# Expert down weights read as one run per partition, hidden units dealt out to tiles with a step of four

## The chip, the cores and the metric

The kernel runs on one core of a Trainium2 chip. The metric is the time of one execution in microseconds (us); the median of three runs counts. Engines are named as the profile names them: PE is TensorE (PEld its weight loads), DVE VectorE, ACT ScalarE, POOL GpSimd, SP SyncE.

## The reference

Two layers work on 256 tokens of width 1024, in float32. A layer is a mixer (one input projection, three kinds of heads, an output projection, a residual) and then a mixture of 32 SwiGLU experts of inner width 512, of which each token uses two. For one expert the reference computes

```
(silu(xb @ w_gate[e]) * (xb @ w_up[e])) @ w_down[e]     # xb (tokens, 1024)
# w_gate[e], w_up[e]: (1024, 512)    w_down[e]: (512, 1024)
```

and the results are summed per token with the router's weights. The sum over the 512 inner units in the last product may be taken in any order, if the activations and the rows of w_down go in the same order.

## The kernel before

All experts are computed, each on up to 32 gathered token rows (CAP = 32). Each expert is a unit; four units (UG = 4) make a group, and a layer has 8 groups. A unit needs three loads of 2 MB: gate, up and down. They go into a ring of six slots in SBUF, three for even units and three for odd ones, so that two units are held at a time. The first four units of a layer borrow other buffers (`FIRST`), and two of the down loads are made in halves (`half_down`).

All loads are issued by SP, in order. `unit` waits until TensorE has done the up part of unit i-2 (`gu_ps`), issues gate and up of unit i, waits until the down part of unit i-2 is done (`ye_ps`), and issues down of unit i. The loads of gate and up take eight neighbouring rows of 512 numbers to a partition, 16 KB in one piece. The load of down takes rows p, 128+p, 256+p and 384+p to partition p, four pieces of 4 KB (L400).

On TensorE, `experts` (L583) runs a group: gather the tokens (L589), turn the weights of the routing (L594), then for each unit the "up" part and the "down" part, and at the end the scatter (L631). The up part (L606) has 8 steps k over the model width and in each four matmuls j side by side: matmul j works on 32 columns of the array and computes 128 inner units, for gate and for up at once. Its moving operand is 2 x 128 numbers, the blocks `P * j:P * j + P` of gate and of up; its output has the 32 tokens on partitions 32j to 32j+31 and the units on 256 columns. ACT and DVE make the activation (L889, L1161 to L1167), TensorE transposes it (L611), ACT copies it to SBUF as `actT` (L892), and the down part (L623) multiplies it: block j of actT with rows j of the down tile, which are those inner units that matmul j has computed. L896 and L1171 copy the result out. The order is "up, down, up, down" in most groups; the first group of a layer has up parts ahead of down parts (`OVERLAPPED`).

Each float32 matmul that is no transpose stands in the trace as two records, one for each of two passes. The 32 matmuls of an up part are 64 records, in 16 steps of four records side by side. TensorE's clock has two levels, 1.2 and 2.4 GHz; the profile gives the granted clock as a share of 2.4 GHz.

The one other strided read on TensorE is in `stream_rows` (L848), which has blocks of x transposed by L580 with a step of 8 numbers (32 bytes) from one element to the next; for the mixer the same line transposes blocks of h, and L696 blocks of q and k, that are contiguous. In these transposes the data are the operand that is loaded as weights.

Of the kernel before, what the change touches and what calls it, by code (L numbers as in the profile page):

```python
# [13 lines left out]
ds = bass.ds  # L14

P = 128
# [40 lines left out]
def hybrid_trunk(nc, a, out):  # L57
# [16 lines left out]
    KT = D // P  # L74
# [30 lines left out]
    with ctx:  # L105
        def sb(name, shape, dt=F32):
            return ctx.enter_context(nc.sbuf_tensor(name, shape, dt))
# [5 lines left out]
        ring = sb("ring", [P, R + 1, SLOT])  # L113
# [129 lines left out]
        def slots_of(i):  # L243

            return (3, 4, 5) if i % 2 == 0 else (0, 1, 2)
# [4 lines left out]
        def slot(s):  # L250
            if s == IN_MAPS:
                return maps[:, :, :].rearrange("p m n -> p (m n)")
            if s == IN_WORK:
                return work[:, 0:8, :].rearrange("p m n -> p (m n)")
            return ring[:, s, :]

        def down_tiles(s, half_in_ht=False):

            tiles = slot(s).rearrange("p (j n) -> p j n", j=4)
            early = hT[:, :, :].rearrange("p (j k) t -> p j (k t)", j=2)  # L260
            return [(early if half_in_ht and j < 2 else tiles)[:, j, :] for j in range(4)]
# [100 lines left out]
        def _(e):  # L362
# [22 lines left out]
            for l in range(DEPTH):  # L385
                for c0, name in ((NE, "group"), (0, "expert")):
                    n = a[f"router_{name}_b"].shape[1]
# [3 lines left out]
            for l in range(DEPTH):  # L391
                w_out = a["w_out"][l:l + 1].rearrange("l (k p) n -> p (l k) n", k=KT)

                def part(full, s, ex, n):

                    if n < 2:
                        src = a[("expert_w_gate", "expert_w_up")[n]][l:l + 1, ds(ex, 1)].rearrange("l e (p k) n -> p (l e k n)", k=KT)
                        e.dma_start(slot(s), src).then_inc(full[s].sem, 16)
                    else:
                        src = a["expert_w_down"][l:l + 1, ds(ex, 1)].rearrange("l e (j p) n -> p (l e j) n", p=P)  # L400
                        e.dma_start(slot(s).rearrange("p (j n) -> p j n", j=4), src).then_inc(full[s].sem, 16)

                def half_down(dst, s, ex, half):

                    src = a["expert_w_down"][l:l + 1, ds(ex, 1)].rearrange("l e (j p) n -> p (l e j) n", p=P)
                    e.dma_start(dst, src[:, 2 * half:2 * half + 2, :]).then_inc(ring_full[s].sem, 16)

                def unit(full, S, turn, i, ex):

                    sg, su, sd = slots_of(i)  # L410
                    e.wait_ge(S.gu_ps.sem, S.gu_ps.after(turn, i - 1))
                    part(full, sg, ex, 0)
                    part(full, su, ex, 1)
                    e.wait_ge(S.ye_ps.sem, S.ye_ps.after(turn, i - 1))
                    part(full, sd, ex, 2)
# [37 lines left out]

                e.wait_ge(log_ps.sem, log_ps.after(l, 1))
                half_down(hT[:, :, :].rearrange("p (j k) t -> p j (k t)", j=2), IN_HT, 3, 0)

                e.wait_ge(main.gu_ps.sem, main.gu_ps.after(first, 1))
# [4 lines left out]
                part(ring_full, FIRST[3][1], 3, 1)  # L462
                e.wait_ge(main.ye_ps.sem, main.ye_ps.after(first, 2))
                half_down(slot(IN_MAPS).rearrange("p (j n) -> p j n", j=4)[:, 2:4, :], IN_MAPS, 3, 1)
                part(ring_full, slots_of(4)[2], 4, 2)
                for i in range(1, UG):
# [6 lines left out]
                with e.If(count > 0):  # L473
                    with e.Fori(0, count) as t:

                        e.wait_ge(main.x_added.sem, main.x_added.after(l * GROUPS + GROUPS - 1, 0))
                        for i in range(UG):
                            ex = e.value_load(xinfo[0:1, l:l + 1, ds(t * UG + (2 + i), 1)], min_val=0, max_val=NE - 1)
# [90 lines left out]
        def _(e):  # L569
# [13 lines left out]
            def experts(S, turn, order, slots_of, loaded):  # L583

                e.wait_ge(S.sel_ok.sem, S.sel_ok.after(turn, 1))
                for half in range(2):
                    for k in range(4):
                        for i in range(TI):
                            last = T.matmul(bank[half][:, k * P:k * P + P], h[:, i, 4 * half + k, :], sel[:, i, :],  # L589
                                            start=(i == 0), stop=(i == TI - 1))  # L590
                    last.then_inc(S.gath_ps.sem, 1)
                e.wait_ge(S.gat_ok.sem, S.gat_ok.after(turn, 1))
                for i in range(TI):
                    last = T.transpose(bank[2][:, i * P:i * P + P], gat[:, i, :], ident[:, :])  # L594
                last.then_inc(S.gat_ps.sem, 1)
                for part, i in order:
                    sg, su, sd = slots_of(i)
                    if part == "up":
                        e.wait_ge(S.full[sg].sem, loaded(sg, i))
                        e.wait_ge(S.full[su].sem, loaded(su, i))  # L600
                        gate_up = ring[:, sg:su + 1:su - sg, :].rearrange("p a (k n) -> p a k n", k=KT)
                        for k in range(KT):
                            if i == 0 and k % 4 == 0:
                                e.wait_ge(S.xg_ok.sem, S.xg_ok.after(turn, 1 + k // 4))
                            for j in range(4):
                                last = T.matmul(bank[GU_BANK[i % 2]][CAP * j:CAP * j + CAP, 0:2 * P], xg[:, k, CAP * i:CAP * i + CAP],  # L606
                                                gate_up[:, :, k, P * j:P * j + P], start=(k == 0), stop=(k == KT - 1))
                        last.then_inc(S.gu_ps.sem, 1)
                        continue
                    e.wait_ge(S.act_ok.sem, S.act_ok.after(turn, i + 1))  # L610
                    T.transpose(bank[3][:, 0:P], actv[i % 2], ident[:, :]).then_inc(S.at_ps.sem, 1)  # L611
                    if i:
                        e.wait_ge(S.ye_act.sem, S.ye_act.after(turn, i))
                        e.wait_ge(S.ye_dve.sem, S.ye_dve.after(turn, i))
                    e.wait_ge(S.full[sd].sem, loaded(sd, i))
                    e.wait_ge(S.at_sb.sem, S.at_sb.after(turn, i + 1))
                    early = order is OVERLAPPED and i == UG - 1
                    if early:
                        e.wait_ge(S.full[IN_HT].sem, loaded(IN_HT, i))
                    down = down_tiles(sd, early)  # L620
                    for j in range(4):
                        for q in range(4):
                            last = T.matmul(bank[5][CAP * q:CAP * q + CAP, 0:2 * P], actT[:, CAP * j:CAP * j + CAP],  # L623
                                            down[j][:, 2 * P * q:2 * P * q + 2 * P], start=(j == 0), stop=(j == 3))
                    last.then_inc(S.ye_ps.sem, 1)
                e.wait_ge(S.gat_sb.sem, S.gat_sb.after(turn, 1))
                e.wait_ge(S.ye_act.sem, S.ye_act.after(turn, 4))
                e.wait_ge(S.ye_dve.sem, S.ye_dve.after(turn, 4))
                for n in range(4):
                    i, half = n // 2, n % 2  # L630
                    T.matmul(bank[(6, 7, 0, 1)[n]][:, :], gatT[:, i * P:i * P + P], ye[:, half * 512:half * 512 + 512],  # L631
                             start=True, stop=True).then_inc(S.scat_ps.sem, 1)

            for l in range(DEPTH):
# [141 lines left out]
                for hd in range(HA):  # L776
                    last = T.matmul(bank[5][:, hd * DV:hd * DV + DV], wT[:, hd, :], av[:, 0, hd * DV:hd * DV + DV],
                                    start=True, stop=True)
# [84 lines left out]
                T.matmul(bank[5][:, 2 * NE:3 * NE], ones[:, :], picks[:, 1, :], start=False, stop=True).then_inc(rank_ps.sem, 1)  # L863

                experts(main, l * GROUPS, OVERLAPPED, lambda i: FIRST[i], lambda s, i: ring_full[s].after(l, 16 * loads(s, i)))
                def turn_loaded(g):
                    return lambda s, i: ring_full[s].after(l, 16 * (loads(s, UG - 1) + i // 2 - 1)) + g * 32

                with e.Fori(1, GROUPS - 1) as g:
                    experts(main, l * GROUPS + g, IN_TURN, slots_of, turn_loaded(g))  # L870
                count, prior = extra_groups(e, l)
                with e.If(count > 0):
                    with e.Fori(0, count) as t:
                        e.wait_ge(main.x_added.sem, main.x_added.after(l * GROUPS + GROUPS - 1, 0))
                        experts(extra, prior + t, IN_TURN, slots_of, lambda s, i: xring_full[s].after(prior + t, 16 * (i // 2 + 1)))
# [737 lines left out]
```

## Time and profile before

| | |
|---|---|
| median of three runs | 1299.38 us (1297.89 to 1301.31) |
| the profiled execution, its own time | 1301.28 us |
| its span in the profile | 1299.5 us |
| mean granted TensorE clock | 0.874 |
| busy: PE, DVE, ACT, POOL | 913.4, 496.4, 183.9, 25.9 us |
| moved by DMA | 442.05 MB in 78306 packets |

Busy times are unions of the records of an engine. A DMA packet is one contiguous piece that one of the 16 DMA engines moves; the profile counts packets under 512 B, under 2 KB and under 8 KB, each count including the smaller ones. The chain that ended last is followed back from the last instruction, at each step to what released it.

### The profile page before, as it was taken

The page shows a single profiled execution, that of the slowest core. Times are in us where ns is not written, and L with a number is a line of the kernel's source. Part 1 is how long each engine was busy: PE and PEld are TensorE (multiplying, and loading weights), DVE is VectorE, ACT ScalarE, POOL GpSimd, SP SyncE. Part 2 cuts the span into 40 slices and gives each one's busy share as a digit, 9 for nine tenths or more (in the row PEclk, how much of TensorE's full clock was granted, in tenths as well). Part 3 has the DMA queues.
Part 4 walks back from the last instruction along what each step waited for, and adds up shares of the span by engine and source line. Part 5 has one row for each costly group of instructions (what it writes and reads, how often), then busy time and mean ns, then how long its engine had stood idle before and what let it go on. Part 6 is the DMA issues. An engine that isn't in the chain of part 4 may idle for free.

```text
span 1299.5 us, 19555 instructions
## 1 busy us (share of the span) xinstructions
PE 913.4 (70%) x8133; PEld 554.1 (43%) x8133; DVE 496.4 (38%) x1245; ACT 183.9 (14%) x544; POOL 25.9 (2%) x63
## 2 busy tenths in 40 slices
PE   5999876667566575656679989757666664665565
PEld 4558453434334343434354574534333342433242
DVE  6666462332323231413147663623323131323222
ACT  2324111110010101110013241010010100010000
POOL 2001000000000000000000020000000000000000
PEclk9999877988888888988689999778878798889888
DMA  7825549899999999999964253498999999999995
GB/s 253 325 97 186 203 163 364 342 420 425 423 422 420 421 424 422 423 423 416 405 241 163 94 205 142 188 397 348 423 422 420 420 423 423 423 423 419 421 422 212
DMA packets 78306, 442.05 MB, mean 340 GB/s; under 512 B 9120, under 2 KB 12208, under 8 KB 61872
## 3 DMA queue, kind: packets, MB, share of 16 engines
q1 hardware_dynamic: 78256, 441.36, 83.7%
q8 instruction: 34, 0.56, 0.2%
q14 instruction: 16, 0.13, 0.0%
HBM read 440.30 MB, written 1.05 MB: 340 GB/s over the span
## 4 chain that ended last, share of the span: by engine, by line
PE 52%; DMA 31%; DVE 11%; issue 2%; ACT 2%; SPq 1%; DVEq 0%; ACTq 0%
DMA ring<-in_expert_w_up 31%; PE bank L606 15%; PE bank L648 8%; PE bank L623 6%; PE bank L657 5%; PE bank L715 4%; PE bank L589 4%; PE bank L631 4%; DVE work L1163 2%; PE bank L679 1%; DVE work L1171 1%; PE bank L580 1%; PE bank L611 1%; ACT work L892 1%; ACT maps L948 1%
## 5 line engine op out<-in xcount | busy, mean ns | idle before, releaser
L606 PE MATMUL bank<-ring,work 128*32 128x256 f32 x4096 | 286.8, 442 | 115.0 <-DMA ring<-in_expert_w_up 114.6
L606 PEld LDWEIGHTS bank<-ring,work 128*32 128x32 f32 x4096 | 163.0, 127 | 236.3 <-issue 161.5
L623 PE MATMUL bank<-ring,work 128*32 128x256 f32 x1856 | 149.6, 477 | 26.6 <-ACT work L892 26.6
L1161 DVE TENSOR_SCALAR work<-work 128x128 f32<-128x128 f32 x64 | 14.5, 227 | 365.8 <-ACT work L889 365.8
L1171 DVE COPY work<-bank 32x256 f32<-32x256 f32 x128 | 54.3, 424 | 206.1 <-PE bank L623 205.2
L611 PE MATMUL bank<-ident,work 128*128 128x128 f32 x64 | 22.4, 349 | 128.4 <-DVE work L1167 128.4
L648 PE MATMUL bank<-ring,hT 128*128 128x512 f32 x256 | 112.4, 593 | 0.0
L623 PEld LDWEIGHTS bank<-ring,work 128*32 128x32 f32 x1856 | 76.7, 133 | 76.6 <-issue 64.1
L589 PE MATMUL bank<-work,h 128*128 128x128 f32 x512 | 73.1, 311 | 40.7 <-DVE work L1141 40.7
L589 PEld LDWEIGHTS bank<-work,h 128*128 128x128 f32 x512 | 70.1, 223 | 52.6 <-DVE work L1141 52.6
L611 PEld LDWEIGHTS bank<-ident,work 128*128 128x128 f32 x64 | 9.3, 145 | 158.6 <-DVE work L1167 156.2
L657 PE MATMUL bank<-hT,ring 128*128 128x256 f32 x320 | 75.3, 397 | 0.8 <-DVE hT L1213 0.8
L631 PE MATMUL bank<-work 128*128 128x512 f32 x128 | 60.9, 620 | 17.2 <-DVE work L1171 17.2
L896 ACT ACTIVATE work<-bank 32x256 f32<-32x256 f32 x128 | 47.8, 373 | 175.1 <-PE bank L623 174.4
L648 PEld LDWEIGHTS bank<-ring,hT 128*128 128x128 f32 x256 | 47.7, 190 | 54.9 <-issue 54.5
L889 ACT ACTIVATE work<-bank 128x128 f32<-128x128 f32 x64 | 17.8, 278 | 356.2 <-PE bank L606 356.2
L657 PEld LDWEIGHTS bank<-hT,ring 128*128 128x128 f32 x320 | 63.4, 200 | 10.6 <-DVE hT L1213 1.2
L1163 DVE RECIPROCAL work<-work 128x128 f32<-128x128 f32 x64 | 61.0, 953 | 2.2
L715 PE MATMUL bank<-ring,hT 128*128 128x512 f32 x128 | 58.1, 610 | 2.8 <-ACT hT L1041 2.8
L1176 DVE TENSOR_TENSOR x<-bank,x 128x512 f32<-128x512 f32 x64 | 44.3, 691 | 30.7 <-PE bank L631 30.7
L631 PEld LDWEIGHTS bank<-work 128*128 128x128 f32 x128 | 23.8, 196 | 49.7 <-issue 49.7
L715 PEld LDWEIGHTS bank<-ring,hT 128*128 128x128 f32 x128 | 24.8, 198 | 32.0 <-issue 32.0
(258 smaller groups left out, 683.6 us busy)
## 6 DMA issues: line engine op xcount, KB each, us to landing
ring<-in_expert_w_gate SPq DMA_DIRECT2D x64, 2048.0 KB, 18.0
ring<-in_expert_w_up SPq DMA_DIRECT2D x64, 2048.0 KB, 22.3
ring<-in_expert_w_down SPq DMA_DIRECT2D x58, 2048.0 KB, 21.9
ring<-in_w_in SPq DMA_DIRECT2D x12, 2048.0 KB, 19.2
ring<-in_w_out SPq DMA_DIRECT2D x4, 2048.0 KB, 8.0
maps<-in_expert_w_down SPq DMA_DIRECT2D x2, 2048.0 KB, 12.7
work<-in_expert_w_down SPq DMA_DIRECT2D x2, 2048.0 KB, 8.3
ring<-in_w_in SPq DMA_DIRECT2D x2, 1024.0 KB, 5.5
```

The costliest lines, as they stand in the source:

```text
L589: last = T.matmul(bank[half][:, k * P:k * P + P], h[:, i, 4 * half + k, :], sel[:, i, :], start=(i == 0), stop=(i == TI - 1))
L606: last = T.matmul(bank[GU_BANK[i % 2]][CAP * j:CAP * j + CAP, 0:2 * P], xg[:, k, CAP * i:CAP * i + CAP], gate_up[:, :, k, P * j:P * j + P] ...
L611: T.transpose(bank[3][:, 0:P], actv[i % 2], ident[:, :]).then_inc(S.at_ps.sem, 1)
L623: last = T.matmul(bank[5][CAP * q:CAP * q + CAP, 0:2 * P], actT[:, CAP * j:CAP * j + CAP], down[j][:, 2 * P * q:2 * P * q + 2 * P], start= ...
L631: T.matmul(bank[(6, 7, 0, 1)[n]][:, :], gatT[:, i * P:i * P + P], ye[:, half * 512:half * 512 + 512], start=True, stop=True).then_inc(S.sc ...
L648: last = T.matmul(bank[b][:, :], hT[:, k, i * P:i * P + P], W[:, k, :], start=(k == 0), stop=(k == KT - 1))
L657: last = T.matmul(bank[b][:, c * SEQ:c * SEQ + SEQ], W[:, k, c0:c0 + P], hT[:, k, :], start=(k == 0), stop=(k == KT - 1))
L715: last = T.matmul(bank[2 * i + half][:, :], mixT[:, k, i * P:i * P + P], W[:, k, :], start=(k == 6), stop=(k == 3))
L896: last = A(ye[CAP * i:CAP * i + CAP, 2 * P * q:2 * P * q + 2 * P], bank[5][CAP * q:CAP * q + CAP, 0:2 * P], ACT.Copy)
L1163: V.reciprocal(r, r).then_inc(c.step(), 1)
L1171: last = V.tensor_copy(ye[CAP * i:CAP * i + CAP, 2 * P * q:2 * P * q + 2 * P], bank[5][CAP * q:CAP * q + CAP, 0:2 * P])
L1176: TT(xs, bank[(6, 7, 0, 1)[n]][:, :], xs, ALU.add).then_inc(S.x_added.sem, 1)
```

## The change

The rows of the down weights go to partitions as 4p, 4p+1, 4p+2 and 4p+3, so that each partition reads 16 KB in one piece (8 KB in the half loads). To match it, matmul j of the up part computes the inner units 4q+j, q = 0 to 127, in place of 128j+q: it reads the gate and up tiles with a step of four numbers (16 bytes). Nothing else differs; no instruction is added or removed on any engine, and gate and up are loaded as before.

```diff
                     else:
-                        src = a["expert_w_down"][l:l + 1, ds(ex, 1)].rearrange("l e (j p) n -> p (l e j) n", p=P)
+                        src = a["expert_w_down"][l:l + 1, ds(ex, 1)].rearrange("l e (p j) n -> p (l e j) n", p=P)
                         e.dma_start(slot(s).rearrange("p (j n) -> p j n", j=4), src).then_inc(full[s].sem, 16)
...
                 def half_down(dst, s, ex, half):
-                    src = a["expert_w_down"][l:l + 1, ds(ex, 1)].rearrange("l e (j p) n -> p (l e j) n", p=P)
+                    src = a["expert_w_down"][l:l + 1, ds(ex, 1)].rearrange("l e (p j) n -> p (l e j) n", p=P)
...
-                        gate_up = ring[:, sg:su + 1:su - sg, :].rearrange("p a (k n) -> p a k n", k=KT)
+                        gate_up = ring[:, sg:su + 1:su - sg, :].rearrange("p a (k n j) -> p a k j n", k=KT, j=4)
...
                                 last = T.matmul(bank[GU_BANK[i % 2]][CAP * j:CAP * j + CAP, 0:2 * P], xg[:, k, CAP * i:CAP * i + CAP],
-                                                gate_up[:, :, k, P * j:P * j + P], start=(k == 0), stop=(k == KT - 1))
+                                                gate_up[:, :, k, j, :], start=(k == 0), stop=(k == KT - 1))
```

## Rows read from the trace of the kernel before

**Rows 1.** The page: engine shares, and DMA in 40 slices of the span.

```profile
PE 913.4 (70%) x8133; PEld 554.1 (43%) x8133; DVE 496.4 (38%) x1245; ACT 183.9 (14%) x544; POOL 25.9 (2%) x63
...
DMA  7825549899999999999964253498999999999995
```

**Rows 2.** The page: the chain that ended last, by engine.

```profile
PE 52%; DMA 31%; DVE 11%; issue 2%; ACT 2%; SPq 1%; DVEq 0%; ACTq 0%
```

**Rows 3.** Windows: the two steady stretches (clock, DMA share, GB/s last).

```profile
254.93:632.71 377.78, 238.83 (x2710) 141.61 (x2711) 107.50 (x252) 35.88 (x109) 0.00 (x0) 0.85 1.01 421
901.00:1277.88 376.88, 237.76 (x2710) 132.89 (x2711) 107.53 (x252) 35.95 (x110) 0.00 (x0) 0.86 1.01 421
```

**Rows 4.** The chain by time (start us, us, what), steady stretch of layer 0.

```profile
374.05 20.00 DMA ring<-in_expert_w_up
...
394.19 5.68 PE bank L606 x64
...
402.90 1.97 PE bank L623 x32
...
417.47 3.63 PE bank L606 x64
...
424.14 1.93 PE bank L623 x32
426.08 3.49 PE bank L606 x64
...
610.36 22.21 DMA ring<-in_expert_w_up
```

**Rows 5.** DMA from 254 to 633 us: packets, then issues with median landing.

```profile
DMA packets 20698, 159.74 MB, mean 421 GB/s; under 512 B 1216, under 2 KB 1216, under 8 KB 14191
...
ring<-in_expert_w_gate SPq DMA_DIRECT2D x25, 2048.0 KB, 18.8
...
ring<-in_expert_w_down SPq DMA_DIRECT2D x25, 2048.0 KB, 22.5
```

**Rows 6.** DMA packets of four windows: 378.5:381.5, 408:412, 384.5:391.5, 414:421.

```profile
DMA packets 300, 1.22 MB, mean 408 GB/s; under 512 B 1, under 2 KB 1, under 8 KB 300
...
DMA packets 400, 1.66 MB, mean 416 GB/s; under 512 B 9, under 2 KB 9, under 8 KB 395
...
DMA packets 200, 3.01 MB, mean 431 GB/s; under 512 B 16, under 2 KB 16, under 8 KB 16
...
DMA packets 197, 2.97 MB, mean 424 GB/s; under 512 B 16, under 2 KB 16, under 8 KB 16
```

**Rows 7.** The chain by time: up parts of layer 0 outside the steady stretch.

```profile
192.26 7.15 PE bank L606 x128
...
219.66 5.90 PE bank L606 x64
...
242.48 3.64 PE bank L606 x64
...
251.09 3.49 PE bank L606 x64
...
632.71 5.88 PE bank L606 x64
```

**Rows 8.** L580 on x and L696: duration ns min/median/max, first and last start.

```profile
L580 PEld LDWEIGHTS bank<-ident,x x32: 188/192/255, 162.6 to 818.1; 128*128 128x128 f32 x32
...
L696 PEld LDWEIGHTS bank<-ident,work x32: 139/141/146, 72.5 to 734.8; 128*128 128x128 f32 x32
L696 PE MATMUL bank<-ident,work x32: 272/272/273, 72.6 to 734.9; 128*128 128x128 f32 x32
```

**Rows 9.** Timeline of PE (start us, us): L696 contiguous, L580 strided.

```profile
89.01 1.04 PE L696 MATMUL bank<-ident,work 128*128 128x128 f32 x8
...
162.74 1.05 PE L580 MATMUL bank<-ident,x 128*128 128x128 f32 x8
...
172.27 1.12 PE L580 MATMUL bank<-ident,x 128*128 128x128 f32 x8
```

## The prediction

> **What bounds the kernel now.** I read the page first. PE is busy for 70% of the span, yet the DMA engines stand at nine tenths or more in two long stretches, one in each layer [rows 1], and the chain that ended last is put down to PE for 52% and to DMA for 31% [rows 2]. A mean over the span doesn't say what a faster load is worth, so I went by stretches. In the two steady stretches, 377.8 and 376.9 us long, the DMA share is 1.01 at 421 GB/s, while PE is busy for 239 and 238 us [rows 3]. In them the loads set the pace: the chain by time goes through a wait for the load of an up weight in each group [rows 4]. Two such loads, 16 units apart, land at 374.05 + 20.00 = 394.05 and at 610.36 + 22.21 = 632.57 us [rows 4], so a unit takes 238.52 / 16 = 14.91 us. It is three loads of 2 MB. SP never lets the queue run dry there: a gate load lands 18.8 us after its issue at the median [rows 5], of which its own transfer is about 5 us, so that some 14 us of other transfers are queued ahead of it.
>
> What PE needs with its data at hand and the clock at 2.4 GHz comes from the same chain. An up part is 3.63 us, and from its end at 421.10 to the end of its down part at 426.07 are 4.97 us. From the end of the last down part of a group (402.90 + 1.97 = 404.87) to the start of the next up part (417.47) are 12.60 us, the scatter and the gather [rows 4]. A group is thus 4 x (3.63 + 4.97) + 12.60 = 47.0 us of PE against 4 x 14.91 = 59.6 us of DMA. PE has some 12.6 us of room in a group.
>
> **The loads.** Each down load is now 512 packets of 4 KB, 32 for each of 16 engines; it becomes 128 of 16 KB, 8 for each, which is what gate and up have. In the stretch there are 25 down loads [rows 5]. Its 12975 packets under 8 KB and not small (14191 - 1216) and 6507 larger ones are the two kinds. What does a packet of each kind cost? A window of 3 us holds 299 of 4 KB on 16 engines: 48 / 299 = 0.1605 us each. One of 4 us holds 386, beside 5 of 16 KB: (64 - 5 x 0.6145) / 386 = 0.158 us. Windows of 7 us hold 184 and 181 of 16 KB, 0.609 and 0.619 us each [rows 6]; two more of that length hold 183 and 181, and the mean of the four is 112 / 182.25 = 0.6145 us. Four small packets are thus 0.632 to 0.642 us against 0.6145 us. After the change a unit is 24 packets of 16 KB on each engine: 24 x 0.6145 = 14.75 us, 0.16 us under 14.91. By the window of 3 us the gain is 8 x (0.642 - 0.6145) = 0.22 us. I take 0.19 us, between the two. The bounds are the two windows of 16 KB: 24 x 0.609 = 14.62 gives 0.29, and 24 x 0.619 = 14.86 gives 0.05 us. With 25 units in each of two stretches [rows 3, 5] that is 50 x 0.19 = **9.5 us**, between 2.5 and 14.5. Each group takes 0.8 us off PE's room of 12.6, so PE doesn't become the bound by this. The down loads outside the stretches, and the halves, lie under other work, and I count nothing for them.
>
> The page "DMA: Bandwidth & Descriptors" of the Trainium skill (Specifications) asks for transfers of at least 512 B for line rate. By it 4 KB pieces would already be at line rate and this gain would be zero; this case's windows show 408 to 416 GB/s with 4 KB pieces and 424 to 431 with 16 KB [rows 6], and they decide. It is the reason why "no gain from the loads" has a chance below.
>
> **The strided read.** Every up part has 16 steps, in each of which four matmul passes read 256 columns side by side: 3.63 us / 16 = 227 ns a step at 2.4 GHz [rows 4]. The step from one element to the next grows from 4 to 16 bytes. No matmul of before reads its moving operand like that. The nearest rows are the transposes of x, whose data are read with a step of 32 bytes as weights. Eight contiguous ones take 1.04 us with 272 ns for one, (1.04 - 0.272) / 7 = 110 ns apart [rows 8, 9]. The strided ones are 111 ns apart in one place and 121 in another [rows 9]. So one stream of elements 32 bytes apart is read at 110 / 128 = 0.86 ns an element with next to no loss, and a moving pass needs 227 / 256 = 0.89 ns an element. That speaks for a cost of zero. Against it are two things. The weight load itself is recorded as 192 ns where the contiguous one has 141 [rows 8], 1.36 times. And an up step reads four such streams at once, which no row shows with a stride. The lower bound is zero, since no row gives a reason for a gain; the upper one is one stream after the other, four times 227 = 908 ns. I take zero, since the spacing, and not the length of one record, is what adds up.
>
> What a longer step costs depends on its place. In a steady stretch PE has 12.6 - 0.8 = 11.8 us a group, 2.9 us an up part, so that the step may grow to 227 + 2900/16 = 410 ns, 1.8 times, before PE is the bound. Outside, the up parts stand on the chain in both layers: 128 records at 192.26, then 64 each at 242.48 and 251.09, all near 2.4 GHz, 64 steps in all [rows 7]. Each ns more a step costs 2 x 64 ns = 0.128 us there. The other two (219.66 and 632.71, 5.90 and 5.88 us, 368 ns a step in the mean since they start on the lower clock) cost something only beyond that.
>
> **The sum.** Loads -9.5, stride 0, issue of the same number of loads 0: 1301.3 - 9.5 = 1291.8 us against the profiled execution's own time. That execution is 1.9 us above the median of the runs, so against the median it is 1289.9, say **1290 us**. Its own range is 1284 to 1297.
>
> **Rivals.** (a) The stride costs 1.3 to 1.5 times, like the record of the weight load. At 1.36 times the step is 309 ns, 0.128 x 82 = 10.5 us more, all outside the steady stretches, where the room hides it. With the gain of the loads that is 1302.3 - 1.9 = 1300 us, no change. What speaks for it is the 192 ns [rows 8], against it the spacing [rows 9].
>
> (b) The other side: four streams of single elements are more than can be read at once, and the step doubles to 454 ns, 7.26 us an up part. This decides from 410 ns on. A group of PE is then 4 x (7.26 + 4.97) + 12.60 = 61.5 us against 59.6 now, 1.9 us more in each of 6.25 groups, 12 us a layer. Outside it are 64 x 227 = 14.5 us a layer, and 1.4 us for each of the two slow ones, 2.8. Together 29 us a layer, 58 in all: 1359.7 - 1.9 = 1358 us. PE, busy without long waits, would hold the clock at 2.4 GHz, so nothing is added for that. At the upper bound of 908 ns a group is 4 x (14.53 + 4.97) + 12.60 = 90.6 us; 6.25 x 31.0 = 194, outside 64 x 0.681 = 43.6 and 2 x 8.6 = 17 us: 255 us a layer, 1810 us. For it speaks that the four streams are untested, against it the single stream at full rate.
>
> The page "SBUF — State Buffer" of the Trainium skill (Specifications; and in "Door 1: The DMA port swizzle") has memory lines of 16 bytes of which at least two accesses must hit each for full bandwidth. With 16 bytes from one element to the next each access is in a line of its own, and by that rule the pass slows, about to (b). The transposes, 32 bytes apart at 111 ns [rows 9], don't show the penalty for one stream; no row shows four.
>
> (c) The loads gain nothing, since the queue's pace is that of the memory and not of the packets, and the stride is free: 1299 us. For it speaks that the windows differ by only 3%, which their ends can blur; against it that each of the four windows of 16 KB gives a higher rate than both of the 4 KB ones shown.
>
> **How the numbers follow.** My forecast has 0.56, (a) 0.11, (c) 0.06, and (b) with all steps above 1.8 times 0.27, of which about half lies at or below twice. The predicted time is that of the likeliest. To leave out no more than 2 in 10 the range has to reach (b) at twice: 1284 to 1362. Beyond lie the upper half of (b), 0.13, and some 0.04 below. A measurement of this kernel can tell 0.3%, 3.9 us, from no change. Faster by more than that is the forecast but for its slow end, 0.54, and a quarter of (a): 0.57. Within it: half of (a), (c) and that slow end: 0.14. Slower: (b) and the rest: 0.29.
>
> **What would show it.** Packets: 32768 of 4 KB go, and 62 x 128 of 16 KB and 4 x 128 of 8 KB come, so 78306 becomes 53986. In the steady stretches GB/s should rise from 421 to about 426, and the landings of up loads 16 units apart should be about 235.5 us apart in place of 238.5. The warm up part (64 records of L606) should stay at 3.63 us. If it reads about 5, (a) holds and the total stands still; at 7.3 and more, (b): the wait of L606 for the up load vanishes from the chain, the DMA share falls under 1, and the granted clock rises. What makes the forecast wrong is above all the four streams side by side.

## The result, and the profile after

The changed kernel takes 1399.43 us in the median of four runs (1398.43 to 1400.08) against 1300.35 us, a ratio of 1.0753, with a 95% interval of 1.0712 to 1.0793. It is slower by 98 us by this ratio (99 by the medians) where 10 us less were forecast, and it lies 37 us beyond the range. Rival (b), the doubled step, named the place; its price of 1358 us was 41 us too low.

The page of the changed kernel: engine shares, granted clock and DMA in 40 slices, packets, and the chain by engine and by line.

```profile
PE 1118.2 (80%) x8133; PEld 563.2 (40%) x8133; DVE 496.4 (36%) x1245; ACT 183.7 (13%) x544; POOL 25.9 (2%) x63
...
PEclk9998989999999998989889989899999998989999
DMA  8826259798998989897953263588998989898973
...
DMA packets 53986, 442.05 MB, mean 316 GB/s; under 512 B 9120, under 2 KB 12208, under 8 KB 29104
...
PE 76%; DVE 14%; ACT 3%; issue 3%; DMA 2%; DVEq 0%; SPq 0%; ACTq 0%
PE bank L606 33%; PE bank L623 13%; PE bank L648 8%; PE bank L589 5%; PE bank L715 4%; PE bank L657 4%; PE bank L631 4%; DVE work L1163 4%; DMA ring<-in_expert_w_up 2%; PE bank L611 1%; ACT work L892 1%; DVE work L1165 1%; DVE work L1167 1%; ACT work L889 1%; DVE work L1171 1%
```

The packets are the 53986 that were worked out, so the loads changed as meant. But DMA has gone from 31% of the chain to 2% [rows 2], and PE's busy time is up by 205 us [rows 1]. The chain by time of the changed kernel shows one whole group, from the first up part to that of the next group.

```profile
443.02 7.45 PE bank L606 x61
...
453.50 1.94 PE bank L623 x32
455.44 7.30 PE bank L606 x64
...
465.78 3.54 PE bank L623 x32
469.32 7.34 PE bank L606 x60
...
479.70 3.42 PE bank L623 x32
483.11 7.31 PE bank L606 x62
...
493.46 3.40 PE bank L623 x32
...
507.83 4.17 PE bank L606 x33
```

An up part takes 7.3 to 7.45 us where the warm one took 3.63 [rows 4], and a group 507.83 - 443.02 = 64.8 us where the loads of four units took 59.6. There is no wait for a load left in it. And there is something that the prediction didn't have: the down part (L623) takes 1.94 us after the first up part and 3.4 to 3.5 after the other three. The windows of the same stretch, an up part, the wait behind one, and the down part behind that, show why (clock, DMA share and GB/s last):

```profile
455.30:462.70 7.40, 7.40 (x68) 2.56 (x60) 0.84 (x2) 0.75 (x2) 0.00 (x0) 1.00 1.01 434
...
463.00:465.70 2.70, 0.33 (x1) 0.14 (x1) 1.76 (x4) 0.31 (x2) 0.00 (x0) 1.00 1.05 449
465.80:469.00 3.20, 3.20 (x32) 1.74 (x36) 0.00 (x0) 0.00 (x0) 0.00 (x0) 0.50 0.98 420
```

The clock is granted in full (1.00) during the up part and the wait, and halved (0.50, the 1.2 GHz level) in the down part behind them. Of the 64 down parts of this kernel 42 take over 2.3 us, of those of the kernel before 25; the sums are 184 and 161 us. The wait itself is in the timeline of PE, 2.29 us ahead of the transpose:

```profile
464.99 0.33 PE L611 MATMUL bank<-ident,work 128*128 128x128 f32 x1 [2.29 <-DVE work L1167]
```

### The profile page after: what moved, and what is told of

It is laid out like the page before. It is cut to its first block, busy times and chain, and to the rows that moved or that the text cites. A ratio compares the mean times of both kernels' runs of the same rounds, so it can differ in the third digit from the quotient of the medians.

```text
span 1397.7 us, 19555 instructions
## 1 busy us (share of the span) xinstructions
PE 1118.2 (80%) x8133; PEld 563.2 (40%) x8133; DVE 496.4 (36%) x1245; ACT 183.7 (13%) x544; POOL 25.9 (2%) x63
## 2 busy tenths in 40 slices
DMA packets 53986, 442.05 MB, mean 316 GB/s; under 512 B 9120, under 2 KB 12208, under 8 KB 29104
## 3 DMA queue, kind: packets, MB, share of 16 engines
HBM read 440.30 MB, written 1.05 MB: 316 GB/s over the span
## 4 chain that ended last, share of the span: by engine, by line
PE 76%; DVE 14%; ACT 3%; issue 3%; DMA 2%; DVEq 0%; SPq 0%; ACTq 0%
PE bank L606 33%; PE bank L623 13%; PE bank L648 8%; PE bank L589 5%; PE bank L715 4%; PE bank L657 4%; PE bank L631 4%; DVE work L1163 4%; DMA ring<-in_expert_w_up 2%; PE bank L611 1%; ACT work L892 1%; DVE work L1165 1%; DVE work L1167 1%; ACT work L889 1%; DVE work L1171 1%
## 5 line engine op out<-in xcount | busy, mean ns | idle before, releaser
L606 PE MATMUL bank<-ring,work 128*32 128x256 f32 x4096 | 478.5, 633 | 7.2 <-DMA ring<-in_expert_w_up 7.2
L606 PEld LDWEIGHTS bank<-ring,work 128*32 128x32 f32 x4096 | 168.5, 128 | 279.6 <-issue 275.7
L623 PE MATMUL bank<-ring,work 128*32 128x256 f32 x1856 | 172.8, 537 | 26.6 <-ACT work L892 26.6
L1161 DVE TENSOR_SCALAR work<-work 128x128 f32<-128x128 f32 x64 | 14.5, 227 | 444.0 <-ACT work L889 444.0
L623 PEld LDWEIGHTS bank<-ring,work 128*32 128x32 f32 x1856 | 84.6, 150 | 91.3 <-issue 85.0
L648 PE MATMUL bank<-ring,hT 128*128 128x512 f32 x256 | 112.4, 593 | 0.0
L589 PE MATMUL bank<-work,h 128*128 128x128 f32 x512 | 69.7, 302 | 41.3 <-DVE work L1141 32.1
L589 PEld LDWEIGHTS bank<-work,h 128*128 128x128 f32 x512 | 66.7, 214 | 53.2 <-DVE work L1141 42.3
L889 ACT ACTIVATE work<-bank 128x128 f32<-128x128 f32 x64 | 17.7, 277 | 434.2 <-PE bank L606 434.2
L715 PE MATMUL bank<-ring,hT 128*128 128x512 f32 x128 | 61.1, 637 | 2.7 <-ACT hT L1041 2.7
```

The source lines that it names most:

```text
L648: last = T.matmul(bank[b][:, :], hT[:, k, i * P:i * P + P], W[:, k, :], start=(k == 0), stop=(k == KT - 1))
L715: last = T.matmul(bank[2 * i + half][:, :], mixT[:, k, i * P:i * P + P], W[:, k, :], start=(k == 6), stop=(k == 3))
```

## The experiments

All ratios are to the kernel before, run on the same chip. Three questions were open: is the gain of the loads real, which reads are slow (four streams at once, any step, or one number to a 16-byte line), and where the 41 us beyond rival (b) went.

**The loads alone.** Only the two down loads change; the up matmuls read as before.

```diff
-                        src = ....rearrange("l e (j p) n -> p (l e j) n", p=P)
+                        src = ....rearrange("l e (p j) n -> p (l e j) n", p=P)      # in part and in half_down
```

> Down weights in 16 KB runs, the up matmuls as before with contiguous reads (so activations meet the wrong rows of the down weights; the work is the same). Theory of the prediction: 50 down loads in the steady stretches save 0.19 us each, 9.5 us in all (2.5 to 14.5), ratio 0.993 (0.989 to 0.998), up loads 16 units apart land about 235.5 us apart. Rival (the pace is that of the memory, not of the packets): ratio 1.000, 238.5 us apart.

The ratio is 0.9926 (0.9897 to 0.9955), 9.6 us off, with an interval of 5.8 to 13.4 (the medians, 1291.43 and 1298.96, are 7.5 apart). The chain by time has these two waits for an up load, 16 units apart:

```profile
375.82 19.18 DMA ring<-in_expert_w_up
...
608.54 21.37 DMA ring<-in_expert_w_up
```

They land at 395.00 and 629.91 us, 234.9 us apart where 238.5 were [rows 4]: 14.68 us a unit, 0.23 less than before, for which 0.19 was taken. The packets of this kernel from 254 to 633 us:

```profile
DMA packets 11157, 162.20 MB, mean 428 GB/s; under 512 B 1236, under 2 KB 1236, under 8 KB 1259
```

428 GB/s against 421 [rows 3, 5], as 14.91/14.68 would have it. Rival (c) falls. The rule of the page "DMA: Bandwidth & Descriptors" of the Trainium skill (Specifications), at least 512 B for line rate, read as if 4 KB pieces had nothing to gain, does not hold to the last 1.6%: the trace shows the smaller pieces slower by that much.

**The strided read alone.** The changed kernel with the down rows still in 4 KB pieces: the four blocks are stored in reverse order, so that neighbouring rows don't join to one run.

```diff
-                        e.dma_start(slot(s).rearrange("p (j n) -> p j n", j=4), src)
+                        e.dma_start(slot(s).rearrange("p (j n) -> p j n", j=4)[:, ::-1, :], src)
...
-                                            down[j][:, ...]
+                                            down[3 - j][:, ...]
```

> The strided up matmuls alone: down weights stay in four 4 KB pieces (rows 4p+j, the four blocks stored in reverse order so that the pieces don't join; TensorE reads them accordingly). If the strided read is the whole loss, PE sets the pace and the loads don't matter: the time is that of the changed kernel, 1396 to 1402 us, with an up part of 7.4 us. If the larger packets had a part in the loss (by holding up PE's reads), an up part gets shorter and the time is under 1390 us.

The ratio is 1.0779 (1.0753 to 1.0805), 1400.32 us. Its groups of instructions have the up part as slow as with the large packets:

```profile
L606 PE MATMUL bank<-ring,work 128*32 128x256 f32 x4096 | 478.8, 633 | 8.0 <-DMA ring<-in_expert_w_up 8.0
```

The whole loss comes with the strided read; once PE sets the pace, the larger packets are worth nothing that can be told (1.0753 and 1.0779, intervals that overlap).

**A step of two.** Pairs of neighbouring rows in 8 KB runs, and matmul j = 2h + b takes the units 256h + 2q + b.

```diff
-                        gate_up = ring[:, sg:su + 1:su - sg, :].rearrange("p a (k n) -> p a k n", k=KT)
+                        gate_up = ring[:, sg:su + 1:su - sg, :].rearrange("p a (k h n b) -> p a k h b n", k=KT, h=2, b=2)
...
-                                                gate_up[:, :, k, P * j:P * j + P], ...)
+                                                gate_up[:, :, k, j // 2, j % 2, :], ...)
```

> A step of two numbers (8 bytes) in place of four: tile j = 2h + b takes inner units 256h + 2q + b, and a partition of the down tile reads two runs of 8 KB. Theory of the 16-byte line (what slows a read is that each number lies in a 16-byte line of its own): two numbers of each line are read by a stream one after the other, so an up part stays at 3.6 us, and the total falls by what the 8 KB packets save, 0 to 10 us, ratio 0.992 to 1.000. Theory of the stride as such (any step that isn't one slows the read): up part near 7.3 us, ratio 1.06 to 1.08. If the cost follows the lines touched per number (a half here, one in the changed kernel, a quarter before), the up part is between, 4.9 us, and the ratio 1.00.

The ratio is 0.9955 (0.9935 to 0.9975), and the mean pass of L606 takes 438 ns, where the one with a step of four has 633 and the contiguous one of the kernel before 442 (second line; both means mix the two levels of the clock):

```profile
L606 PE MATMUL bank<-ring,work 128*32 128x256 f32 x4096 | 283.3, 438 | 104.4 <-DMA ring<-in_expert_w_up 104.4
...
L606 PE MATMUL bank<-ring,work 128*32 128x256 f32 x4096 | 286.8, 442 | 115.0 <-DMA ring<-in_expert_w_up 114.6
```

The median pass takes 388 ns against 379 in the kernel before. A stride as such costs next to nothing here; a number to each 16-byte line is another matter.

**A table of reads.** The kernel before, with series of 16 matmuls behind its last scatter, each behind 24 contiguous ones.

```diff
+            def wide_4():
+                for n in range(16):
+                    T.matmul(bank[3][:, :], stat[:, 0:P], moving(4, 512, n), start=True, stop=True)
...
+            def four_4():
+                for n in range(16):
+                    for j in range(4):
+                        T.matmul(bank[3][CAP * j:CAP * j + CAP, 0:2 * P], stat[:, 0:CAP],
+                                 ring[:, 0:2, j % 4:j % 4 + 4 * (P - 1) + 1:4], start=True, stop=True)
```

> The kernel before, and behind its last scatter a series of matmuls on what lies in SBUF, 16 of each kind with 24 contiguous ones ahead of each kind: full width with 512 columns, 128-byte and other steps 1, 2, 3, 4 and 8; four side by side with 2 x 128 columns, same steps; one of 32 columns alone, steps 1 and 4; the strided operand as weights, steps 1 and 4. Nothing is left out of the kernel; its total says nothing, the rows of the series do. At 2.4 GHz, theory of four streams (too many reads at once): step 4 costs nothing for one stream (427 ns for two passes of 512 columns), twice for four. Theory of the 16-byte line: step 4 and 8 take twice, 853 ns, already for one stream, step 2 takes 427, step 3 lies at or between. As weights, step 4: no more than 111 ns apart for 128 columns if moving and loaded operand differ. Then three long series (64 steps of four strided, 64 of four contiguous, 64 of one wide strided): if the strided read lowers the clock, the granted clock falls in the first and the third while PE is busy without a gap, and stays at 1.0 in the second; if the clock follows the gaps only, it stays at 1.0 in all three.

In the timeline of PE (start us, us) the full-width series with steps 1, 2, 3, 4 and 8 are L889, L893, L897, L901 and L905; four side by side are L910, L915, L920, L925 and L930; 32 columns alone with steps 1 and 4 are L938 and L934; a contiguous and a strided operand loaded as weights are L942 and L946.

```profile
1314.01 13.90 PE L889 MATMUL bank<-ring,work 128*128 128x512 f32 x32
...
1348.34 14.56 PE L893 MATMUL bank<-ring,work 128*128 128x512 f32 x32
...
1383.34 21.76 PE L897 MATMUL bank<-ring,work 128*128 128x512 f32 x32
...
1425.54 28.96 PE L901 MATMUL bank<-ring,work 128*128 128x512 f32 x32
...
1474.94 29.57 PE L905 MATMUL bank<-ring,work 128*128 128x512 f32 x32
...
1525.05 7.11 PE L910 MATMUL bank<-ring,work 128*32 128x256 f32 x128
...
1613.13 14.84 PE L925 MATMUL bank<-ring,work 128*32 128x256 f32 x128
...
1684.38 7.09 PE L938 MATMUL bank<-ring,work 128*32 128x256 f32 x32
...
1712.20 14.60 PE L934 MATMUL bank<-ring,work 128*32 128x256 f32 x32
...
1747.43 3.73 PE L942 MATMUL bank<-work,ring 128*128 128x128 f32 x32
...
1771.61 7.50 PE L946 MATMUL bank<-work,ring 128*128 128x128 f32 x32
...
1799.64 58.40 PE L925 MATMUL bank<-ring,work 128*32 128x256 f32 x512
```

Against the contiguous series, step 2 costs 1.05 times, step 3 1.57, step 4 2.08 and step 8 2.13. (One pass of 512 columns takes 13.90/32 = 0.43 us; the expectation had this for two, and the first one on filling the wait, below, has the same error.) Four streams are no worse than one: 14.84/7.11 = 2.09 side by side, and 14.60/7.09 = 2.06 for one narrow stream alone. The theory of four streams falls. The strided operand loaded as the weights of an ordinary matmul costs double too. That is the rule of the page "SBUF — State Buffer" of the Trainium skill (Specifications), at least two accesses to each 16-byte line for full bandwidth, and this case's rows agree: step 2 has two, steps 4 and 8 have one, and step 3 with 1.33 lies between. The factors follow twice the lines touched per number, once that is over 1: step 3 touches three lines for four numbers, 2 x 0.75 = 1.5 against 1.57 measured, steps 4 and 8 one for each number, 2 against 2.08 and 2.13.

The long series of strided reads, 64 steps in 58.40 us, kept the clock. Its window:

```profile
1799.70:1858.00 58.30, 58.30 (x514) 1.00 0.00 1
```

So in a series without gaps the strided reads didn't lower the clock.

**The row that misled.** The transposes, in three series of 32.

```diff
+                for n in range(32):
+                    T.transpose(bank[3][:, 0:P], ring[:, 0, n % 4:n % 4 + 4 * (P - 1) + 1:4], ident[:, :])
```

> The kernel before, and behind its last scatter three series of 32 transposes of 128 x 128 numbers in SBUF with steps 1, 4 and 8 between the elements, each behind 24 contiguous matmuls. This is the row on which the prediction leaned, repeated in a long series. If transposes read strided data at full rate, where matmul passes don't, all three are 110 to 121 ns apart. If the eight transposes in the trace of before were too few to show the cost, steps 4 and 8 are about 220 ns apart.

Steps 1, 4 and 8 in the timeline of PE:

```profile
1308.12 3.66 PE L889 MATMUL bank<-ident,ring 128*128 128x128 f32 x32
...
1332.21 4.02 PE L896 MATMUL bank<-ident,ring 128*128 128x128 f32 x32
...
1356.68 3.75 PE L903 MATMUL bank<-ident,ring 128*128 128x128 f32 x32
```

Taking off the 0.27 us of the last, they are 109, 121 and 112 ns apart. The row of before [rows 9] was read rightly: a transpose reads strided numbers at nearly full pace, a tenth slower with step 4 and hardly slower with step 8. But it is no measure of a matmul, whose weights with a step of 4 are (7.50 - 0.40)/31 = 229 ns apart against (3.73 - 0.28)/31 = 111. A float32 transpose is one record where a float32 matmul is two; why the one doesn't slow is not settled.

**Filling the wait.** The changed kernel with contiguous matmuls into an unread bank while PE waits for the activation, first four and then two of them in each unit.

```diff
+                    if i == 0:
+                        e.wait_ge(S.gat_sb.sem, S.gat_sb.after(turn, 1))
+                    for n in range(4):      # 2 in the second version
+                        T.matmul(bank[2][:, :], h[:, 0, 0, :], h[:, 0, 4:8, :], start=True, stop=True)
                     e.wait_ge(S.act_ok.sem, S.act_ok.after(turn, i + 1))
```

> The changed kernel with four more matmuls (128 x 128 by 512 contiguous columns, 1.73 us at 2.4 GHz) into a bank that nobody reads, put on PE in each unit in the 2.3 us in which it waits for the activation. The work of the reference is complete. Theory of the clock (beyond the doubled up part, the change loses time since the down part behind it runs at 1.2 GHz, 3.4 us in place of 1.9, as the engine sat idle before it): with the idle time filled the down parts go back to 1.9 to 2.0 us, a group from 64.8 to about 62 us, and the total from 1399 to 1345 to 1370 us. Rival (the down part is slow for another reason, for one the loads that write the ring at the same time): nothing gained, 1399 us or more.

> As the first filler, with two matmuls in place of four. The first one showed the pass of 512 columns at 0.45 us, so that four matmuls took 3.63 us, more than the 2.3 us of idle time, and held up the path by 1.3 us a unit, while each down part was back at 1.93 us. Two take 1.8 us and fit. Theory of the clock: down parts stay at 1.9 to 2.0 us, a group takes 62 us in place of 64.8, and the total is 1345 to 1370 us. Rival (that much work isn't enough to hold the clock, or the time was not lost to it): the down parts are at 3.4 us again in most units, 1395 to 1402 us.

With four the ratio is 1.0903 (1.0874 to 1.0932), 1415.91 us, slower than the changed kernel: the four take 3.63 us, more than the wait. But the down parts are fast again, all of them. With two the ratio is 1.0439 (1.0417 to 1.0462), 1355.89 us. The chain by time of the version with two, a group from its first up part to the next group's (L627 is the down part):

```profile
434.68 7.40 PE bank L606 x64
...
445.11 1.93 PE bank L627 x32
447.05 7.32 PE bank L606 x62
...
457.40 1.93 PE bank L627 x32
...
469.71 1.93 PE bank L627 x32
...
482.00 1.97 PE bank L627 x32
...
494.94 5.08 PE bank L606 x41
```

This group takes 60.3 us in place of 64.8. It is one of the three shortest; most others take 61.8 to 62.0, like the one ahead of it:

```profile
372.83 7.45 PE bank L606 x61
...
420.17 1.97 PE bank L627 x32
434.68 5.52 PE bank L606 x45
```

The 1.6 us between the two kinds lie in the gather (L589), which takes 3.84 us at the full clock and some 5.4 behind this group, where the clock is at 0.69. So the two matmuls keep the clock up in the down parts, and in most groups some of it is lost in the gather instead. One gather of this execution, at 606 us, also stands idle some 7 us longer than its like in the others, with nothing in the trace that released it. The two groups of instructions, of the changed kernel and of the filled one:

```profile
L623 PE MATMUL bank<-ring,work 128*32 128x256 f32 x1856 | 172.8, 537 | 26.6 <-ACT work L892 26.6
```

```profile
L627 PE MATMUL bank<-ring,work 128*32 128x256 f32 x1856 | 112.2, 381 | 26.6 <-ACT work L896 26.6
```

Work that computes nothing takes 43.5 us off the changed kernel by the medians, 41 by the ratios (1.0753 - 1.0439). No other change was made, and the down parts alone are 184.4 - 123.8 = 60.6 us shorter in sum, part of which is lost again in the gathers. So 41 to 43.5 us, net, of the changed kernel's time go with the clock, and what is left, 1355.9 us, is close to what rival (b) had worked out, 1358.

**The loads without the strided read.** The units are dealt out on DVE. It writes the activation with unit 4r + j of a block in column 32j + r, and turns it in blocks of 32 x 32, which puts unit 4q + j on partition q of block j, where the 16 KB load has its row. The transpose on PE and ACT's copy go, and `actT` has two buffers.

```diff
-                        TT(actv[i % 2], gu[:, P:2 * P], r, ALU.mult).then_inc(S.act_ok.sem, 1)
+                        TT(actv[i % 2].rearrange("p (j r) -> p r j", j=4), gu[:, P:2 * P].rearrange("p (r j) -> p r j", j=4),
+                           r.rearrange("p (r j) -> p r j", j=4), ALU.mult).then_inc(c.step(), 1)
+                        e.wait_ge(c.sem, c.last())
+                        V.transpose(actT[i % 2], actv[i % 2]).then_inc(S.at_sb.sem, 1)
```

> The 16 KB loads without any strided read on TensorE: the up matmuls read contiguous blocks as before, DVE writes the activation with its columns dealt out (unit 4r + j of a block to column 32j + r) and turns it in blocks of 32 x 32, which puts unit 4q + j on partition q of block j; the transpose on TensorE and ACT's copy fall away. The loads alone gave a ratio of 0.9926. If DVE's turn costs 0.2 to 0.4 us, it saves about as much of the 0.86 us from activation to down part, on the chain in some 10 units: 2 to 5 us. Expected: up part 3.6 us, ratio 0.987 to 0.993. Rival: DVE reads and writes with a step as slowly as TensorE does, the chain gets longer, ratio 0.993 to 0.997.

> The same with down weights in 4 KB pieces (blocks stored in reverse order). Tells the part of the packets from that of the shorter chain: if the packets are worth 9.5 us here too, ratio 0.7% above that of the 16 KB version, 0.995 to 1.000.

With 16 KB runs the ratio is 0.9926 (0.9901 to 0.9951), 1289.47 us against 1300.49; with 4 KB pieces 0.9987 (0.9971 to 1.0002). The packets are worth 0.6%, about 8 us, here too. The shorter chain is worth nothing that can be told; the 2 to 5 us expected of it don't show. DVE's part in the timeline:

```profile
425.13 0.37 DVE L1162 TENSOR_TENSOR work<-bank,work 128x128 f32<-128x128 f32 x1
425.53 0.31 DVE L1165 STREAM_TRANSPOSE work<-work 128x128 f32<-128x128 f32 x1
425.90 0.20 PEld L621 LDWEIGHTS bank<-ring,work 128*32 128x32 f32 x8 [3.21 <-DVE work L1165]
425.90 3.26 PE L621 MATMUL bank<-ring,work 128*32 128x256 f32 x32 [2.73 <-DVE work L1165]
```

The product with strided reads and writes takes 0.37 us, 0.08 more than the contiguous one, and the turn 0.31. Here the down part runs mostly at the lower clock, 3.26 us, where the one before [rows 4] took 1.93. Of the kernels that compute the whole reference this is the fastest, level with the loads alone.

## Why the prediction was wrong

**What bounds the kernel** was read rightly: the loads set the pace of the steady stretches, and a step of 410 ns was about the point from which PE would be the bound. One term was misread. The 12.60 us for scatter and gather were put under "the clock at 2.4 GHz", but the gather in them ran at 0.69 (first line, the kernel before); at the full clock (second line, the changed kernel) it is 3.84 us in place of 5.47, and scatter and gather are 507.83 - 496.86 = 10.97.

```profile
411.80:417.30 5.50, 5.50 (x34) 5.43 (x34) 1.66 (x6) 0.00 (x0) 0.00 (x0) 0.69 1.03 433
```

```profile
503.80:507.70 3.90, 3.90 (x34) 3.80 (x34) 1.68 (x6) 0.00 (x0) 0.00 (x0) 1.00 0.99 420
```

PE's room was thus up to 1.6 us larger, and the step could have grown to some 435 ns. The measured step, 7.3/16 = 456 ns, is past that too, and PE is the bound.

**The loads.** Forecast 9.5 us, between 2.5 and 14.5; measured alone 9.6 us (ratio 0.9926), with 0.23 us a unit where 0.19 was taken. This step holds, both in its cause and its size; that the two agree to 0.1 us is luck, since the measurement leaves 5.8 to 13.4. In the changed kernel no gain can be seen, since another engine sets the pace.

**The step that failed** is "I take zero, since the spacing, and not the length of one record, is what adds up". The spacing was that of transposes, and the table of reads shows that the transposes are the exception: each other read in it with a step of 16 or 32 bytes takes about twice the time (2.01 to 2.13), moving or loaded, one stream or four. The up part went from 3.63 to 7.3 us, a term that the sum had at nothing. The weight on the untested four streams was misplaced too; they cost no more than one. The page's rule of the 16-byte lines, which stood beside it in the prediction, gave the right answer, and the row held against it was from another operation.

**Rival (a)** falls: no read slowed by the 1.36 of one record.

**Rival (b)** is what happened, though not for its reason: one stream alone is doubled like four. Its step of 454 ns was measured at 456, its up part of 7.26 us at 7.3 to 7.45. Its price failed in one sentence, "PE, busy without long waits, would hold the clock at 2.4 GHz, so nothing is added for that". The waits of 2.3 us for the activation remain in each unit, and behind them three of four down parts ran at 1.2 GHz. The miss of 41 us lies in the steady groups: they take 64.8 us where 61.5 were worked out, and 3.3 us in 12.5 groups are 41. Three slow down parts add 1.60 + 1.48 + 1.46 = 4.5 us, the gather, warm here, takes 1.6 away, and up parts and waits add 0.4. Outside these groups (98 - 65)/2 = 16.5 us a layer are left, for which 17 were worked out. With the wait filled the time is 1355.9 us: 41 to 43.5 us of the loss go with the clock, and 55 to 57 are left, for which 58 were worked out. That this comes so close is in part luck, since with the filler the gather is at the lower clock in most groups, as in the 12.60 us from which (b) was added up. Why this wait costs the clock behind a strided up part more often than it did behind a contiguous one (42 down parts of 64 against 25) isn't settled: in the long series without gaps the strided reads kept the clock, and before the change warm down parts stood behind the same waits [rows 4].

**The range** ended at 1362 since (b) was priced without the clock. With it, 1400 us would have been inside a range that reached (b).

## What to carry to other kernels

Have each stream that a float32 matmul reads take at least two numbers from each 16-byte line: here a step of two was nearly free (1.05), a step of four doubled the time (2.08), and only the transposes were spared. A row of the trace bounds a cost only for the same operation; here the nearest row was of another one, and the rule that spoke against it was right. Where a change makes PE the bound, its short waits come onto the path with the clock that they cost: price the work behind each wait at both clock levels.

## What was not expected of the hardware

A float32 transpose of data 16 bytes apart runs at 121 ns, while the same data as weights of a matmul take 229 (contiguous 109 and 111). DMA packets of 16 KB move 428 GB/s where a mix with two thirds of the packets at 4 KB moved 421. And 1.8 us of useless matmuls in each 12 us unit made the changed kernel 41 to 43.5 us faster, with all 64 down parts at the 2.4 GHz level (mean granted clock 0.963 in place of 0.922).
